# Expert rounds of 96 token places in place of 128, in a one-core decoder step on Trainium2

## The chip, the cores and the metric

The kernel runs on one core of one Trainium2 chip. The core has a matmul engine (TensorE, "PE" in the profile, its weight loads "PEld"), a vector engine (VectorE, "DVE"), a scalar engine (ScalarE, "ACT"), GpSimd ("POOL") and the engine that issues most of the transfers (SyncE, "SP"); 16 DMA engines move the data. The metric is the device time of one execution in microseconds, the median of three runs.

## What is computed

One inference step of a two-layer decoder, in float32, for 256 prompt tokens and 8 sample tokens (264 in all), model width 1024. Layer 0 is a gated DeltaNet mixer and a dense SwiGLU; layer 1 is a short gated convolution and a top-2-of-8 expert SwiGLU. The change is in the experts:

```python
def moe_swiglu(x, w_router, w_gu, w_down):
    logits = (x @ w_router).astype(jnp.float32)            # (tokens, 8)
    top_v, top_i = lax.top_k(logits, 2)
    gates = jax.nn.softmax(top_v, axis=-1)
    combine = jnp.einsum('...k,...ke->...e', gates, jax.nn.one_hot(top_i, 8, dtype=jnp.float32))
    y = jnp.zeros_like(x)
    for e in range(8):                                      # w_gu[e]: 1024 x 7168, w_down[e]: 3584 x 1024
        y = y + swiglu(x, w_gu[e], w_down[e]) * combine[..., e:e + 1].astype(x.dtype)
    return y
```

Each token goes to two experts, so an expert serves 66 tokens on average. The router of this reference, evaluated on its inputs, sends 68, 81, 87, 70, 66, 53, 45 and 58 tokens to the eight experts.

## The kernel before

Every weight matrix is streamed once, in slots of 128 x 2048 floats (1 MB). SP loads a slot into one of seven buffers (`raw`, line 360); ACT rounds it to the matmul format (`high`, line 367); DVE takes the remainder (`low`, line 372) over the raw data. A product is then three matmuls: high weights by high data, high by low, low by high. PE's `slot_used` semaphore gives the buffers back.

In layer 0 and in the convolution the weights are the stationary operand and all 264 tokens (266 columns) stream past. In the experts it is turned round: the tokens are the stationary operand (128 x CAP) and the weights stream past, 512 columns at a time.

The expert part works in *rounds*. A round gives each expert CAP places, CAP = 128; the number of rounds is read from the largest token count (`most`, lines 1632 to 1639: one, plus one if it is above CAP, plus one if above 2 CAP), and every round runs all eight experts. One expert in one round is a *job*: 42 slots, the same instruction stream on each engine, looped over with `Fori`, with the last job written out. The order inside a job is fixed by hand. A job has seven units of 512 hidden features (`UNITS`). For each unit PE does

- `gate_or_up` twice (lines 2279 to 2296): 48 matmuls, stationary `xgh` or `xgl` (128 x CAP), moving `high` or `low` (128 x 512), result in banks 0 to 3,
- `transpose_hidden` (line 2303): four transposes of `hx` (CAP x 128 each) into bank 6 or 7, the data as stationary operand and the identity as moving operand; they stand between the gate and the up half of the next unit,
- `down` (lines 2306 to 2327): 24 matmuls, stationary a CAP-column slice of `hth` or `htl`, moving `high` or `low`, accumulated in banks 4 and 5.

ACT applies silu (`sgx`, line 1061) and copies the transposed hidden tile (`hth`, line 1055); DVE multiplies (`hx`, line 1720) and takes the remainder (`htl`, line 1710). Near the end of a job `transpose_rows` (line 2260) transposes the next expert's tokens, eight transposes of `xrow`; DVE (`xf`, line 1644; `xgl`, line 1650) and ACT (`xgh`, line 1044) prepare them.

Tokens reach their places in two ways. For the first expert a one-hot matrix is built on DVE (line 1610) and 24 products with `xn` gather the columns (line 2268, each recorded as two matmuls). For the others POOL scatters rows into a DRAM table `tok` of 26 blocks of CAP rows (line 708), which SP reads back block by block (line 531). SP also stores each job's result `ysb` there (line 526). The 26 blocks are set to zero in layer 0 by transfers that POOL issues (line 610). After the last job POOL gathers each token's two results, except those of the last expert, which are taken from SBUF by a product with `final_ohT`.

## Time and profile before

| | us |
|---|---|
| median of three runs (1536.56 to 1539.73) | 1537.85 |
| span of the profiled execution | 1533.9 |
| PE busy in it | 1512.4 (99%) |
| PE weight loads busy | 1323.3 |
| DVE busy | 1274.1 (83%) |
| ACT busy | 1036.4 (68%) |
| POOL busy | 110.7 |
| mean granted clock of TensorE | 0.999 of full speed |

The span runs from the first to the last instruction of the profiled execution; the 3.95 us between it and the median lie around it. The experts run from about 561 us to about 1514 us of the span. In the timeline a line such as "x4" merges four neighbouring instructions: its start is that of the first and its length runs to the end of the last. The length of a single matmul includes the time until its result is out; neighbouring matmuls overlap. What one costs in a stream is the distance from its start to the start of the next.

### The profile page before, as it was taken

Reading aid. Unit: us, or ns where it says so; the run is one execution under the profiler, and the core shown is the slowest. Engines: PE = TensorE matmul, PEld = TensorE weight load, DVE = VectorE, ACT = ScalarE, POOL = GpSimd, SP = SyncE. Lnnn points to the kernel's source line nnn. Section 1 sums busy time; section 2 is a strip of 40 time slices with the busy share of each in tenths; the row PEclk is TensorE's granted clock in tenths of the full one; section 3 lists DMA queues with packets and bytes.
Section 4 is the critical chain, followed back from the end, with each engine's and each line's share of the span. In section 5 each row is a group of like instructions: output and inputs, shape, how many; then the busy total and the mean of one; then the engine's idle time right before and its main releaser. Section 6 shows DMA issues by size and latency. Waiting matters only on the chain.

```text
span 1533.9 us, 24252 instructions
## 1 busy us (share of the span) xinstructions
PE 1512.4 (99%) x9241; PEld 1323.3 (86%) x9241; DVE 1274.1 (83%) x1328; ACT 1036.4 (68%) x974; POOL 110.7 (7%) x171
## 2 busy tenths in 40 slices
PE   9999999999999999999999999999999999999997
PEld 8899999999999988888888888888888888888885
DVE  6986557796458779999899889889889889889896
ACT  6872546665344457777778778778778778777773
POOL 4313000120030120000000000000000000002100
PEclk9999999999999999999999999999999999999999
DMA  9968026896555559999999999999999999999991
GB/s 310 354 231 309 3 97 193 273 318 212 190 180 180 167 189 400 379 364 395 384 358 392 386 363 381 393 371 381 386 376 377 388 372 375 389 374 368 411 409 57
DMA packets 228140, 476.80 MB, mean 311 GB/s; under 512 B 10165, under 2 KB 69669, under 8 KB 227770
## 3 DMA queue, kind: packets, MB, share of 16 engines
q1 hardware_dynamic: 216216, 435.66, 77.9%
q0 software_dynamic: 11856, 40.19, 7.4%
q8 instruction: 48, 0.79, 0.2%
q14 instruction: 20, 0.16, 0.0%
HBM read 449.80 MB, written 26.24 MB: 310 GB/s over the span
## 4 chain that ended last, share of the span: by engine, by line
PE 90%; DVE 5%; ACT 3%; issue 2%; DVEq 0%; ACTq 0%
PE bank L2295 13%; PE bank L2291 12%; PE bank L2292 12%; PE bank L410 12%; PE bank L2320 11%; PE bank L416 6%; PE bank L2326 6%; PE bank L2156 3%; DVE low L372 2%; PE bank L2303 2%; PE bank L2161 1%; ACT high L367 1%; DVE xf L1644 1%; PE bank L423 1%; PE bank L432 1%
## 5 line engine op out<-in xcount | busy, mean ns | idle before, releaser
L372 DVE TENSOR_TENSOR low<-raw,high 128x2048 fp32r<-128x2048 f32 x404 | 919.9, 2292 | 142.4 <-ACT high L367 139.1
L367 ACT ACTIVATE high<-raw 128x2048 fp32r<-128x2048 f32 x404 | 773.6, 1918 | 284.3 <-PE bank L2295 89.0
L2291 PE MATMUL bank<-high,xgh 128*128 128x512 f32 x896 | 354.2, 395 | 0.4 <-DVE xgl L1650 0.4
L2292 PE MATMUL bank<-high,xgl 128*128 128x512 f32 x896 | 350.1, 391 | 0.0
L2295 PE MATMUL bank<-low,xgh 128*128 128x512 f32 x896 | 241.4, 392 | 1.4 <-DVE low L372 1.1
L2295 PEld LDWEIGHTS bank<-low,xgh 128*128 128x128 f32 x896 | 167.7, 188 | 40.3 <-DVE low L372 5.2
L2291 PEld LDWEIGHTS bank<-high,xgh 128*128 128x128 f32 x896 | 168.6, 188 | 34.2 <-issue 0.5
L2292 PEld LDWEIGHTS bank<-high,xgl 128*128 128x128 f32 x896 | 168.5, 188 | 33.8
L410 PE MATMUL bank<-xhb,high 128*128 128x266 f32 (+1 forms) x752 | 155.6, 288 | 2.0 <-DVE utail L1196 1.9
L410 PE MATMUL bank<-xlb,high 128*128 128x266 f32 (+1 forms) x752 | 153.9, 286 | 0.0
L2320 PE MATMUL bank<-high,hth 128*128 128x512 f32 x448 | 139.6, 393 | 0.0
L2320 PE MATMUL bank<-high,htl 128*128 128x512 f32 x448 | 138.2, 390 | 0.0
L410 PEld LDWEIGHTS bank<-xhb,high 128*128 128x128 f32 x752 | 117.3, 189 | 3.9 <-DVE utail L1196 2.1
L2326 PE MATMUL bank<-low,hth 128*128 128x512 f32 x448 | 120.0, 390 | 0.0
L410 PEld LDWEIGHTS bank<-xlb,high 128*128 128x128 f32 x752 | 117.6, 189 | 0.0
L416 PE MATMUL bank<-xhb,low 128*128 128x266 f32 (+1 forms) x752 | 101.7, 288 | 0.0
L2320 PEld LDWEIGHTS bank<-high,htl 128*128 128x128 f32 x448 | 84.2, 188 | 17.6
L2326 PEld LDWEIGHTS bank<-low,hth 128*128 128x128 f32 x448 | 84.1, 188 | 17.7 <-DVE low L372 0.2
L2320 PEld LDWEIGHTS bank<-high,hth 128*128 128x128 f32 x448 | 83.0, 188 | 16.3
L416 PEld LDWEIGHTS bank<-xhb,low 128*128 128x128 f32 x752 | 96.1, 190 | 1.1 <-issue 1.0
L722 POOL TENSOR_TENSOR flag<-flag 128x1 f32<-128x1 f32 x1 | 0.9, 873 | 840.7 <-DMA tok<-ysb 840.7
L1061 ACT ACTIVATE sgx<-bank 128x512 f32<-128x512 f32 x56 | 33.5, 598 | 38.4 <-PE bank L2295 38.2
(460 smaller groups left out, 1527.0 us busy)
## 6 DMA issues: line engine op xcount, KB each, us to landing
raw<-in_moe_w_gu_dram SPq DMA_DIRECT2D x224, 1024.0 KB, 5.6
raw<-in_moe_w_down_dram SPq DMA_DIRECT2D x112, 1024.0 KB, 6.0
raw<-in_ffn_w_gu_dram SPq DMA_DIRECT2D x22, 1024.0 KB, 5.6
raw<-in_gdn_w_in_dram SPq DMA_DIRECT2D x16, 1024.0 KB, 12.5
tok<-zeros POOLq DMA_DIRECT2D x26, 512.0 KB, 9.7
raw<-in_sc_w_in_dram SPq DMA_DIRECT2D x12, 1024.0 KB, 4.9
raw<-in_ffn_w_down_dram SPq DMA_DIRECT2D x11, 1024.0 KB, 5.5
s<-in_state_gdn_S_dram POOLq DMA_DIRECT2D x8, 512.0 KB, 8.0
```

Of the source, the lines that this page charges most:

```text
L367: eng.activation(high[:, n % SPLIT, :], raw[:, n % RAW, :], ACT.Copy).then_inc(high_ready, 1)
L372: eng.tensor_tensor(low[:, n % RAW, :], raw[:, n % RAW, :], high[:, n % SPLIT, :].bitcast(F32), ALU.subtract).then_inc(low_ready, 1)
L410: pe.matmul(out[t], wh[:, k, f[t]], act_[:, k, :], start=k == 0 and act_ is act_h, stop=False)
L416: last = pe.matmul(out[t], wl[:, k, f[t]], act_h[:, k, :], start=False, stop=k == KT - 1)
L1061: act.activation(sgx[:, u % 2, :], bank[2 * (u % 2)][:, :], ACT.Silu).then_inc(sgx_ready, 1)
L2156: pe.matmul(bank[d][:, 0:N], wh[:, k, 128 * d:128 * d + 128], act_[:, f + k, :], start=f + k == 0 and act_ is hh, stop=False)
L2291: pe.matmul(out, xgh[:, 4 * kh + k, :], wh[:, k, :], start=kh + k == 0, stop=False)
L2292: pe.matmul(out, xgl[:, 4 * kh + k, :], wh[:, k, :], start=False, stop=False)
L2295: last = pe.matmul(out, xgh[:, 4 * kh + k, :], wl[:, k, :], start=False, stop=kh == 1 and k == 3)
L2303: last = pe.transpose(bank[6 + u % 2][:, 128 * q:128 * q + 128], hx[:, u % 2, 128 * q:128 * q + 128], idn)
L2320: pe.matmul(bank[4 + g][:, :], src[:, u % 2, hs], wh[:, k, 512 * g:512 * g + 512], start=u + kh + k == 0 and src is hth, stop=False)
L2326: last = pe.matmul(bank[4 + g][:, :], hth[:, u % 2, hs], wl[:, k, 512 * g:512 * g + 512], start=False, stop=u == UNITS - 1 and kh + k == 2)
```

## The change

CAP goes from 128 to 96. Tiles that have a token on their partitions lose their last 32 partitions, tiles that have a token on their columns have 96 of them, and the transposes take a 96 x 96 identity. The number of rounds follows from the same comparison, now with 96 and 192. There are still at most three rounds, so 24 job blocks and two spare ones in `tok`.

```diff
-CAP = 128
+CAP = 96
 TILES = -(-N // CAP)
...
-        hx = place("hx", [128, 2, 512], at=region + 24 * D)
-        sgx = place("sgx", [128, 2, 512], at=region + 28 * D)
-        hth = place("hth", [128, 2, 512], F32R, at=region + 32 * D)
-        htl = place("htl", [128, 2, 512], F32R, at=region + 36 * D)
-        ysb = place("ysb", [128, D], at=region + 40 * D)
-        xrow = place("xrow", [128, D], at=region + 44 * D)
+        hx = place("hx", [CAP, 2, 512], at=region + 24 * D)
+        sgx = place("sgx", [CAP, 2, 512], at=region + 28 * D)
+        hth = place("hth", [128, 2, 4 * CAP], F32R, at=region + 32 * D)
+        htl = place("htl", [128, 2, 4 * CAP], F32R, at=region + 36 * D)
+        ysb = place("ysb", [CAP, D], at=region + 40 * D)
+        xrow = place("xrow", [CAP, D], at=region + 44 * D)
...
                     pool.dma_start(tok[j].rearrange("p (h f) -> p h f", h=4),
-                                   zeros[:, :].rearrange("p (o f) -> p o f", o=1).to_broadcast([128, 4, 256])).then_inc(zero_out, 16)
+                                   zeros[0:CAP, :].rearrange("p (o f) -> p o f", o=1).to_broadcast([CAP, 4, 256])).then_inc(zero_out, 16)
...
-                    act.activation(hth[:, u % 2, :], bank[6 + u % 2][:, :], ACT.Copy).then_inc(hth_ready, 1)
+                    act.activation(hth[:, u % 2, :], bank[6 + u % 2][:, 0:4 * CAP], ACT.Copy).then_inc(hth_ready, 1)
...
-                            act.activation(sgx[:, u % 2, :], bank[2 * (u % 2)][:, :], ACT.Silu).then_inc(sgx_ready, 1)
+                            act.activation(sgx[:, u % 2, :], bank[2 * (u % 2)][0:CAP, :], ACT.Silu).then_inc(sgx_ready, 1)
...
-                    ins = dve.tensor_scalar(xf[:, d, :], heads(2 + g)[:, d % 4, :], vecs[:, d, 2:3], vecs[:, d, 6:7],
+                    ins = dve.tensor_scalar(xf[:, d, :], heads(2 + g)[:, d % 4, 0:CAP], vecs[:, d, 2:3], vecs[:, d, 6:7],
                                             ALU.mult, ALU.add)
...
-                    dve.tensor_tensor(htl[:, u % 2, :], bank[6 + u % 2][:, :], hth[:, u % 2, :].bitcast(F32),
+                    dve.tensor_tensor(htl[:, u % 2, :], bank[6 + u % 2][:, 0:4 * CAP], hth[:, u % 2, :].bitcast(F32),
                                       ALU.subtract).then_inc(htl_ready, 1)
...
-                        last = pe.transpose(heads(2 + g)[:, d, :], xrow[:, ds], idn)
+                        last = pe.transpose(heads(2 + g)[:, d, 0:CAP], xrow[:, ds], ident[0:CAP, 0:CAP])
...
-                        last = pe.matmul(heads(2 + g)[:, d % 4, :], xn[:, tt, 128 * d:128 * d + 128], onehot[:, tt, :],
+                        last = pe.matmul(heads(2 + g)[:, d % 4, 0:CAP], xn[:, tt, 128 * d:128 * d + 128], onehot[:, tt, :],
                                          start=tt == 0, stop=tt == 2)
...
-                    out = bank[2 * (u % 2) + w][:, :]
+                    out = bank[2 * (u % 2) + w][0:CAP, :]
...
-                        last = pe.transpose(bank[6 + u % 2][:, 128 * q:128 * q + 128], hx[:, u % 2, 128 * q:128 * q + 128], idn)
+                        last = pe.transpose(bank[6 + u % 2][:, CAP * q:CAP * q + CAP], hx[:, u % 2, 128 * q:128 * q + 128],
+                                            ident[0:CAP, 0:CAP])
...
-                            hs = slice(256 * kh + 128 * k, 256 * kh + 128 * k + 128)
+                            hs = slice(CAP * (2 * kh + k), CAP * (2 * kh + k) + CAP)
                             for src in (hth, htl):
                                 for g in range(2):
-                                    pe.matmul(bank[4 + g][:, :], src[:, u % 2, hs], wh[:, k, 512 * g:512 * g + 512],
+                                    pe.matmul(bank[4 + g][0:CAP, :], src[:, u % 2, hs], wh[:, k, 512 * g:512 * g + 512],
                                               start=u + kh + k == 0 and src is hth, stop=False)
```

The tiles `onehot`, `xf`, `xgh`, `xgl`, `final_oh` and `seat` have CAP columns by their declarations, so they shrink with the constant.

## Rows read from the trace of the kernel before

**Rows 1.** The page, busy time by engine: us, share of the span, instructions.

```profile
PE 1512.4 (99%) x9241; PEld 1323.3 (86%) x9241; DVE 1274.1 (83%) x1328; ACT 1036.4 (68%) x974; POOL 110.7 (7%) x171
```

**Rows 2.** Windows in the experts: us, busy (instructions) by engine, granted clock, DMA share, GB/s.

```profile
1000.00:1100.00 100.00, 99.95 (x456) 82.53 (x455) 90.99 (x59) 77.28 (x53) 0.00 (x0) 1.00 1.02 381
```

**Rows 3.** Waits of PE, 560 to 1500 us: who waited for whom, us, times, longest.

```profile
PE bank L2295 <- DVE low L372: 1.1, 2, 0.6
PE bank L2291 <- DVE xgl L1650: 0.4, 1, 0.4
```

**Rows 4.** Waits of the load queue and of ACT, 600 to 1500 us.

```profile
SPq L360 <- PE bank L2295: 448.3, 210, 2.9
SPq L360 <- PE bank L2326: 232.8, 106, 3.0
...
ACT high L367 <- DMA raw<-in_moe_w_gu_dram: 5.2, 8, 0.7
```

**Rows 5.** Timeline of PE, a slot of gate_or_up: start us, length us, instruction, forms.

```profile
1014.10 0.39 PE L2291 MATMUL bank<-high,xgh 128*128 128x512 f32 x1
...
1015.91 1.07 PE L2295 MATMUL bank<-low,xgh 128*128 128x512 f32 x4
1016.82 0.39 PE L2291 MATMUL bank<-high,xgh 128*128 128x512 f32 x1
```

**Rows 6.** Groups by form, weight loads: rows*columns of the load, count, busy us, mean ns.

```profile
L2291 PEld LDWEIGHTS bank<-high,xgh 128*128 128x128 f32 x896 | 168.6, 188 | 34.2 <-issue 0.5
...
L1971 PEld LDWEIGHTS bank<-T,AT 64*64 64x64 f32 x320 | 9.9, 135 | 1.2 <-issue 1.0 <-ACT Kn L873 0.2
...
L1912 PEld LDWEIGHTS bank<-xhb,wabh 128*40 128x40 f32 x8 | 0.9, 114 | 0.1
```

**Rows 7.** Timeline of PE, 264 columns past a stationary operand 40 wide.

```profile
19.46 0.28 PE L1912 MATMUL bank<-xlb,wabh 128*40 128x264 f32 x1
...
22.12 0.29 PE L1912 MATMUL bank<-xhb,wabl 128*40 128x264 f32 x1
```

**Rows 8.** The same past a stationary operand 128 wide.

```profile
539.13 0.28 PE L423 MATMUL bank<-yh,high 128*128 128x264 f32 x1
...
540.73 0.28 PE L424 MATMUL bank<-yl,high 128*128 128x264 f32 x1
```

**Rows 9.** Timeline of PE around one transpose_hidden, and what follows it.

```profile
1018.64 1.07 PE L2295 MATMUL bank<-low,xgh 128*128 128x512 f32 x4
1019.55 0.60 PE L2303 MATMUL bank<-ident,hx 128*128 128x128 f32 x4
1019.90 0.48 PE L2291 MATMUL bank<-high,xgh 128*128 128x512 f32 x1
1020.22 0.40 PE L2292 MATMUL bank<-high,xgl 128*128 128x512 f32 x1
```

**Rows 10.** The chain of work, pieces of the two kinds of transposes: start us, us.

```profile
671.51 0.44 PE bank L2303 x4
...
674.72 0.87 PE bank L2260 x8
```

**Rows 11.** Transposes of 11 stationary columns by 128 moving ones: timeline, then its loads.

```profile
233.96 1.91 PE L2119 MATMUL bank<-ident,utail 128*11 128x128 f32 x16
...
L2119 PEld LDWEIGHTS bank<-ident,utail x24: 91/93/93, 233.7 to 358.1; 128*11 128x11 f32 x24
L2119 PE MATMUL bank<-ident,utail x24: 270/273/273, 234.0 to 358.2; 128*11 128x128 f32 x24
```

**Rows 12.** Transposes of 128 stationary columns by 28 moving ones: timeline, then one.

```profile
17.71 1.67 PE L1906 MATMUL bank<-ident,taps_nat 28*128 28x28 f32 x24
...
L1906 PE MATMUL bank<-ident,taps_nat x24: 217/218/240, 17.7 to 19.2; 28*128 28x28 f32 x24
```

**Rows 13.** One line's instructions: the token transposes of seven jobs, and the hidden ones.

```profile
L2260 PE MATMUL bank<-ident,xrow x56: 270/273/273, 674.6 to 1389.0; 128*128 128x128 f32 x56
...
L2303 PE MATMUL bank<-ident,hx x224: 269/272/277, 578.6 to 1505.2; 128*128 128x128 f32 x112
```

**Rows 14.** Timeline, start of the experts: the gather, and DVE, ACT and PE behind it.

```profile
555.31 5.62 PE L2268 MATMUL bank<-onehot,xn 128*128 128x128 f32 x48
...
559.70 0.63 ACT L1044 ACTIVATE xgh<-xf 128x512 fp32r<-128x512 f32 x1 [4.38 <-DVE xf L1644]
560.36 0.69 DVE L1650 TENSOR_TENSOR xgl<-xf,xgh 128x512 fp32r<-128x512 f32 x1 [0.70 <-ACT xgh L1044]
560.98 1.37 DVE L1644 TENSOR_SCALAR xf<-bank,vecs 128x128 f32<-128x128 f32 x4
...
561.29 0.49 PE L2291 MATMUL bank<-high,xgh 128*128 128x512 f32 x1 [0.36 <-DVE xgl L1650]
```

**Rows 15.** Timeline of PE: float32 matmuls with 8 moving columns, no transposes.

```profile
548.96 1.23 PE L2202 MATMUL bank<-gbw,xres 128*128 128x8 f32 x16
550.12 3.25 PE L2212 MATMUL bank<-high 128*128 128x512 f32 x13
```

**Rows 16.** Groups by form, DVE and ACT, of the hidden tile.

```profile
L1710 DVE TENSOR_TENSOR htl<-bank,hth 128x512 fp32r<-128x512 f32 x56 | 38.2, 682 | 0.0
...
L1055 ACT ACTIVATE hth<-bank 128x512 fp32r<-128x512 f32 x56 | 33.3, 595 | 9.9 <-PE bank L2303 9.9
```

More of the change, by code:

```diff
@@ L247, in hybrid_step @@
         final_oh = place("final_oh", [128, 3, CAP], at=region + 90 * D)
-        final_ohT = place("final_ohT", [128, N], at=tab_at + 4864)
+        final_ohT = place("final_ohT", [CAP, N], at=tab_at + 4864)
         quarters = place("quarters", [128, 3, 4, 6], at=region + 90 * D + 1600)
@@ L253, in hybrid_step @@
         SROWS = 4 * NS
-        seat_win = place("seat_win", [128, 40], at=mask_at)
+        seat_win = place("seat_win", [CAP, 40], at=mask_at)
         row_win = place("row_win", [128, 40], at=mask_at + 160)
@@ L1068, in expert @@
                         act.wait_ge(y_stored, job * 16 + 16)
-                        act.activation(ysb[:, 0:512], bank[4][:, :], ACT.Copy).then_inc(y_sb, 1)
+                        act.activation(ysb[:, 0:512], bank[4][0:CAP, :], ACT.Copy).then_inc(y_sb, 1)
                     if not last or i + SPLIT < EXPERT_SLOTS:
@@ L1719, in expert @@
                             dve.wait_ge(sgx_ready, units + (u + 1))
-                            dve.tensor_tensor(hx[:, u % 2, :], sgx[:, u % 2, :], bank[2 * (u % 2) + 1][:, :],
+                            dve.tensor_tensor(hx[:, u % 2, :], sgx[:, u % 2, :], bank[2 * (u % 2) + 1][0:CAP, :],
                                               ALU.mult).then_inc(hx_ready, 1)
@@ L1728, in expert @@
                             dve.wait_ge(ohT_psum, 1)
-                            step(dve.tensor_copy(final_ohT[:, :], bank[2][:, 0:N]))
+                            step(dve.tensor_copy(final_ohT[:, :], bank[2][0:CAP, 0:N]))
                             step(dve.tensor_copy(seat_win[:, 0:SROWS].rearrange("p (b d) -> p b d", d=4)[:, :, 3:4],
-                                                 bank[2][:, NP:N].rearrange("p (b o) -> p b o", o=1)))
+                                                 bank[2][0:CAP, NP:N].rearrange("p (b o) -> p b o", o=1)))
                             step.wait()
@@ L1736, in expert @@
                         dve.wait_ge(y_stored, job * 16 + 16)
-                        dve.tensor_copy(ysb[:, 512:1024], bank[5][:, :]).then_inc(y_sb, 1)
+                        dve.tensor_copy(ysb[:, 512:1024], bank[5][0:CAP, :]).then_inc(y_sb, 1)
                     if not last or i + SPLIT < EXPERT_SLOTS:
@@ L2323, in down @@
                         for k in range(2):
-                            hs = slice(256 * kh + 128 * k, 256 * kh + 128 * k + 128)
+                            hs = slice(CAP * (2 * kh + k), CAP * (2 * kh + k) + CAP)
                             for g in range(2):
-                                last = pe.matmul(bank[4 + g][:, :], hth[:, u % 2, hs], wl[:, k, 512 * g:512 * g + 512],
+                                last = pe.matmul(bank[4 + g][0:CAP, :], hth[:, u % 2, hs], wl[:, k, 512 * g:512 * g + 512],
                                                  start=False, stop=u == UNITS - 1 and kh + k == 2)
@@ L2345, in expert @@
                         n_tok = 128 if tt < 2 else NS
-                        last = pe.transpose(bank[2][:, 128 * tt:128 * tt + n_tok], final_oh[0:n_tok, tt, :], ident[0:n_tok, 0:n_tok])
+                        last = pe.transpose(bank[2][0:CAP, 128 * tt:128 * tt + n_tok], final_oh[0:n_tok, tt, :], ident[0:n_tok, 0:n_tok])
                     last.then_inc(ohT_psum, 1)
```

## The prediction

> **What bounds the kernel now.** I read the page first: PE is busy for 99% of the span, the next engine for 83% [rows 1]. A pipelined matmul counts as busy until its result is out, so that share doesn't say that PE is at its peak. The windows over the experts are alike from 600 to 1500 us: PE 99.95, DVE 91, ACT 77, granted clock 1.00, which is the 2.4 GHz level [rows 2]. The list of waits settles it: between 560 and 1500 us PE stood still for 1.5 us in all [rows 3]. The load queue, in contrast, waits for PE to give slots back for 681 us, and ACT waits only 5.2 us for the gate and up weights [rows 4]. So in the experts only the time that PE spends in its own instructions counts. A saving on DVE, ACT or in the transfers is worth nothing there by itself.
>
> What one instruction costs is the distance between starts. A gate slot has 12 matmuls of 512 columns and runs from 1014.10 to 1016.82, 2.72 us: 227 ns each [rows 5]. At 2.4 GHz 512 columns are 213 ns, so 14 ns are lost per matmul. A job has 42 such slots: 504 x 0.227 = 114.4 us. The job period is 118.9 us: from 674.6 to 1389.0 are seven groups of eight token transposes [rows 13], less the 0.76 us inside one group (seven distances of 0.109), over six periods. The rest, about 4.5 us, is 28 + 8 transposes and a little slack.
>
> **How many rounds.** The number of jobs comes first. The largest token count is 87, which is below 96, so there is one round of eight jobs as before. The 224 hidden transposes are 8 x 28 [rows 13]: one round today.
>
> **The large matmuls.** All 4032 (8 x 504) keep their 512 moving columns; only the stationary operand is narrower. Its load gets shorter: 188 ns at 128 columns, 135 at 64, 114 at 40 [rows 6], a line of 0.83 ns a column, so about 161 ns at 96. But the load runs beside the matmul ahead of it, and 188 is already less than 227. Does the lost 14 ns depend on the width? I compare 264 moving columns: past 40 stationary columns, 22 distances from 19.46 to 22.12, 121 ns [rows 7]; past 128, 13 distances from 539.13 to 540.73, 123 ns [rows 8]. Two ns for 88 columns is 0.7 ns for 32 columns, or 2.9 us over 4032 matmuls. I take 0 and keep 2.9 us as the bound on the gain side. On the loss side, the slices of stationary operand now begin every 384 bytes instead of 512. The 40-column slices begin every 160 bytes and cost nothing extra, so I take 0 there too, with 0.5 ns (2 us) as the bound.
>
> The Trainium skill, "TensorE: Matmul & The Clock Gate", section "LDWEIGHTS (loading the stationary operand)", says that a load takes P / 1.2 ns with P the columns; the slope of 0.83 in [rows 6] agrees. If the loads were exposed, that would be an estimated 27 ns on each of 4032 matmuls, over 100 us. They aren't, by the 227 ns of [rows 5].
>
> **The transposes.** Here the moving operand is the identity, so its width goes from 128 to 96. The stationary operand stays 128 columns wide (now 96 rows deep). Which of the two sets the time? First what one costs: one group of four starts at 1019.55, and the second matmul behind it at 1020.22; without the group that matmul would be 0.227 us behind, so four transposes cost 0.44 us [rows 9]. The chain of work gives the same 0.44, and 0.87 for eight [rows 10]: 109 ns each. With 11 stationary columns and 128 moving, 16 take 1.91 us; less the 0.273 us of the last one, that is 15 distances of 109 ns [rows 11]. So the narrow load changed nothing. With 128 stationary and 28 moving, 24 take 1.67 us; less 0.218, that is 23 distances of 63 ns [rows 12]. So the load (or another floor) stands at 63 ns, and above it the moving columns decide: 109 ns for 128 is 0.85 ns a column, near two cycles of 2.4 GHz (0.83). At 96 columns: 96 x 0.83 = 80 ns, and the remaining 2 ns, so 82 ns, above the floor of 63. The saving is 27 ns each. In the path stand 8 x 28 = 224 and 7 x 8 = 56 of them [rows 13]: 280 x 0.027 = 7.5 us. The bounds: a straight line between the two measured points (63 at 28, 109 at 128) has 94 ns at 96 columns, a saving of 15 ns or 4.1 us; if the load decided at full width the saving would be 0. I take 7.5, since the row with the 11 stationary columns has the same 109.
>
> The Trainium skill, same page, section "Back-to-back issue gap", gives N / 2.4 + 2.5 ns for a warm matmul, one cycle a column. By it a transpose would cost 56 ns now and 42 after, and 280 of them save an estimated 3.7 us. The 109 ns of [rows 10, 11] speak against it for float32 transposes.
>
> **The start of the experts.** The gather is 48 matmuls whose moving one-hot has 96 columns after the change. They cost (5.62 - 0.28) / 47 = 114 ns each [rows 14], where 0.28 is an estimate for the length of the last one, near the 0.27 of a transpose [rows 13]. Their stationary operand is float32 and 128 wide, and not a transpose. 16 matmuls of that kind, some with a narrower load, run from 548.96 to 550.12, 73 ns each, though only 8 columns stream past [rows 15]. So a full-width load sets at least 73 ns there, and may set all of the 114. The bounds for the 48 are 0 and 48 x 27 ns = 1.3 us; I take 0, because the loads stay at full width. Behind it PE waits 0.36 us for `xgl` [rows 14]. Four `xf` (1.37 us), `xgh` (0.63) and `xgl` (0.69) work on 96 of 128 columns each; a quarter of the streaming part, about 0.1 us of each, comes off, so that wait goes: 0.36 us. The 0.6 us wait for `low` a few slots later [rows 3] hangs on the same DVE queue, which is ahead by two such sets then, some 0.6 us; I take half, 0.3. Sum for the start: 0.7 us, bounds 0 and 2.3.
>
> **What costs nothing, and its cover.** `hth` on ACT (595 ns) and `htl` on DVE (682 ns) [rows 16] stream 384 in place of 512 columns and get shorter by a hundred ns or so, 56 times each; the matmuls between the transposes and `down` cover them entirely today (neither is among PE's waits [rows 3]), and they still do with a group of transposes that is 0.11 us shorter. `sgx`, `hx` and `ysb` have fewer partitions and the same columns, so the same time. The zeroing, the stores of `ysb` and the reads of `xrow` carry 384 KB in place of 512 KB; PE waits for none of them. No wait is added on any queue, and nothing is moved past anything else. Should the cover of the transfers fail, the wait of ACT for weights would grow from its 5.2 us [rows 4]; PE asks for each slot 0.8% sooner.
>
> **The sum.** 7.5 + 0.7 = 8.2 us off the span of 1533.9, hence 1525.7; the 3.95 us around it stay, and the median goes from 1537.85 to 1529.6, 0.5% less.
>
> **The rivals.**
>
> *A. The load holds the transposes.* At full width of both operands load and stream could be equally long, and only the load stay. For it: the load is still 128 columns. Against it: 63 ns with 128 stationary columns [rows 12]. Gain 0.7 us, time 1537.1. Chance 7%.
>
> *B. A transposed column costs less than I take.* Either a floor rises with the width (the straight line above, 4.1 us), or the 32 columns cost what a column of a large matmul does: 227 / 512 = 0.44 ns [rows 5], 14 ns for 32, 280 x 0.014 = 4.0 us. For it: no row has 96 moving columns. Against it: 0.85 ns a column at 128 [rows 11]. Gain 4.0 + 0.7, time 1533.1. Chance 8%.
>
> The back-to-back rule of the Trainium skill quoted above is this case.
>
> *C. Slower: the large matmuls pay for the odd slices.* Place: weight loads of `xgh`, `hth` and the like, at 384-byte steps, and results that fill 96 of 128 partitions. Each ns is 4.0 us, so 2 ns cancel the gain, and from 2.8 ns (11.3 us) it is slower by over 0.2%. At 4 ns: 16.1 - 8.2 = 7.9 us slower, time 1545.8. Against it: no penalty at 160-byte steps [rows 7]. Chance 4%.
>
> *D. A second round.* Price 8 x 118 = 944 us, time about 2470, decided by one expert above 96 tokens. With 87 it needs the kernel's routing to differ in ten places. Chance 1%.
>
> *E. The gain is absorbed.* DMA share is 1.02 at 381 GB/s [rows 2]; if that were the ceiling, PE would wait for weights as much as it saves. Against it: the queue's 681 us of waits [rows 4]. Time 1537.8. Chance 4%.
>
> *F. The large matmuls gain too*, up to 0.7 ns: gain up to 8.2 + 2.9, time 1526.7. Chance 8%.
>
> **How the numbers follow.** The forecast has 68%. Faster by over 0.2% (3.1 us, about what a measurement of this kernel can tell from no change): forecast, B and F, 84%, less 2% for runs that differ among themselves by 0.1% or so: 82%. Within 0.2%: A, E and these 2%, and 1% from a small C: 14%. Slower: 4%, C's larger part and D. The range reaches down to F, less 1 us: 1526. Upward it takes in B and the spread of the runs: 1534.5. A, C, D and E stay out, 16%.
>
> **What would show it.** Transposes on line 2303: four in the path cost 0.33 us in place of 0.44, and eight on line 2260 0.66 in place of 0.87. The job period goes from 118.9 to 118.0. A gate slot is still 2.72 us; loads on line 2291 have a mean near 161 ns. PE's wait for `xgl` is gone. The prediction is wrong if the group of four stays at 0.44 (A), if it comes to 0.38 (B), if a gate slot is off 2.72 by 0.03 or more (C, F), or if there are 16 jobs (D).

## The result, and the profile after

The changed kernel takes 1542.19 us (median of ten runs, 1540.66 to 1544.45) against 1537.35 of the kernel before (ten runs beside them, 1534.95 to 1539.77): ratio 1.0033, 95% interval 1.0024 to 1.0041. It is slower by some 5 us where 8 us less were forecast, and lies outside the stated range. Among the runs behind the numbers below, one of the six of the second experiment (1865.1 us) and one of the kernel before (1582.6 us) had a low granted clock, 0.751 and 0.90; the ratios leave them out, and without the first the median of the second experiment is 1526.99 us in place of 1527.32.

The page of the changed kernel; it answers to [rows 1]. It has the same number of instructions, so there is still one round of eight jobs.

```profile
span 1538.9 us, 24252 instructions
...
PE 1519.0 (99%) x9241; PEld 1211.1 (79%) x9241; DVE 1263.4 (82%) x1328; ACT 1028.2 (67%) x974; POOL 111.5 (7%) x171
```

DVE, ACT and the weight loads all have less to do, as the diff says, and PE is busy for longer. PE doesn't wait more than before; its waits between 560 and 1500 us have become shorter than [rows 3], and this is the only one left:

```profile
PE bank L2295 <- DVE low L372: 0.5, 1, 0.5
```

So the time went into PE's own instructions. The transposes did what was forecast. The chain of work of the changed kernel, the two kinds of transposes, beside [rows 10]:

```profile
663.87 0.33 PE bank L2303 x4
...
675.64 0.66 PE bank L2260 x8
```

0.33 in place of 0.44 and 0.66 in place of 0.87. The groups by form of the changed kernel show the weight loads with the forecast mean of 161 ns:

```profile
L2291 PEld LDWEIGHTS bank<-high,xgh 128*96 128x96 f32 x896 | 144.4, 161 | 60.7
```

Its token transposes, by line, run from 675.5 to 1393.9:

```profile
L2260 PE MATMUL bank<-ident,xrow x56: 243/246/247, 675.5 to 1393.9; 96*128 96x96 f32 x56
```

The job period is (1393.9 - 675.5 - 0.58) / 6 = 119.64 us against 118.94 before, by the same sum (a group of eight is 7 x 0.083 = 0.58 long now). It grew by 0.70 us where it should have shrunk by 0.97. The timeline shows where, in a gate slot as in [rows 5]:

```profile
1017.07 0.39 PE L2291 MATMUL bank<-high,xgh 128*96 128x512 f32 x1
...
1019.85 0.39 PE L2291 MATMUL bank<-high,xgh 128*96 128x512 f32 x1
```

The slot takes 2.78 us in place of 2.72: 231.7 ns for each of its 12 matmuls, with the same 512 moving columns, 5.0 ns more than the 226.7 of the slot before. The average over a job is less. Of the 3967 distances between neighbouring large matmuls in each trace, those up to 245 ns (all but 84 before and 67 after, which stand at transposes and waits) have a mean of 227.4 ns before and 231.4 after: 4.0 ns, or 16 us over 4032 matmuls. That is the size of rival C, which had 4%. What the narrow, shifted loads do to the stream is the subject of the experiments.

There is a second, smaller surprise, in the other direction. Before, the first slot of a job was late. The timeline of the kernel before, DVE and then PE at the change of jobs:

```profile
676.63 2.63 DVE L1644 TENSOR_SCALAR xf<-bank,vecs 128x128 f32<-128x128 f32 x8
679.18 1.47 DVE L1650 TENSOR_TENSOR xgl<-xf,xgh 128x512 fp32r<-128x512 f32 x2
680.57 4.48 DVE L372 TENSOR_TENSOR low<-raw,high 128x2048 fp32r<-128x2048 f32 x2
...
680.89 0.39 PE L2291 MATMUL bank<-high,xgh 128*128 128x512 f32 x1
...
682.48 0.39 PE L2292 MATMUL bank<-high,xgl 128*128 128x512 f32 x1
682.91 1.20 PE L2295 MATMUL bank<-low,xgh 128*128 128x512 f32 x4
683.94 0.39 PE L2291 MATMUL bank<-high,xgh 128*128 128x512 f32 x1
```

The slot takes 3.05 us, 0.33 more than its neighbours: between 682.48 and 682.91 PE waits for `low`, which DVE delivers late after eight `xf` and two `xgl`. The list of waits doesn't count this, since the long record of the matmul before covers the gap. The same place in the changed kernel:

```profile
677.44 2.37 DVE L1644 TENSOR_SCALAR xf<-bank,vecs 128x96 f32<-128x96 f32 x8
679.73 1.23 DVE L1650 TENSOR_TENSOR xgl<-xf,xgh 128x384 fp32r<-128x384 f32 x2
...
681.68 0.39 PE L2291 MATMUL bank<-high,xgh 128*96 128x512 f32 x1
...
684.46 0.39 PE L2291 MATMUL bank<-high,xgh 128*96 128x512 f32 x1
```

2.78 us, an ordinary slot of that kernel. DVE's work there is 0.5 us shorter and the stall of 0.3 us is gone.

The account of one job, in us: transposes -0.97, stall -0.3, and so the 504 large matmuls must bring +0.70 + 0.97 + 0.3 = +2.0, which is 3.9 ns each and agrees with the 4.0 of the distances. Eight jobs give 8 x 0.70 = 5.6 us; the spans differ by 5.0.

### The profile page after: what moved, and what is told of

Its sections match the earlier page's. It is cut to its first block, busy times and chain, and to the rows that moved or that the text cites. A ratio compares the mean times of both kernels' runs of the same rounds, so it can differ in the third digit from the quotient of the medians.

```text
span 1538.9 us, 24252 instructions
## 1 busy us (share of the span) xinstructions
PE 1519.0 (99%) x9241; PEld 1211.1 (79%) x9241; DVE 1263.4 (82%) x1328; ACT 1028.2 (67%) x974; POOL 111.5 (7%) x171
## 4 chain that ended last, share of the span: by engine, by line
PE 95%; DVE 2%; ACT 2%; issue 1%; DVEq 0%; ACTq 0%
PE bank L2321 13%; PE bank L2295 13%; PE bank L2291 13%; PE bank L2292 13%; PE bank L410 12%; PE bank L2327 7%; PE bank L416 6%; PE bank L2156 3%; PE bank L2161 1%; PE bank L2303 1%; PE bank L423 1%; PE bank L432 1%; PE bank L1971 1%; PE bank L424 1%; PE bank L2001 1%; ACT high L367 1%
## 5 line engine op out<-in xcount | busy, mean ns | idle before, releaser
L2291 PE MATMUL bank<-high,xgh 128*96 128x512 f32 x896 | 356.1, 397 | 0.0
L2292 PE MATMUL bank<-high,xgl 128*96 128x512 f32 x896 | 352.1, 393 | 0.0
L2295 PE MATMUL bank<-low,xgh 128*96 128x512 f32 x896 | 243.8, 394 | 0.5 <-DVE low L372 0.5
L2295 PEld LDWEIGHTS bank<-low,xgh 128*96 128x96 f32 x896 | 144.2, 161 | 62.1 <-DVE low L372 0.9
L2291 PEld LDWEIGHTS bank<-high,xgh 128*96 128x96 f32 x896 | 144.4, 161 | 60.7
L2292 PEld LDWEIGHTS bank<-high,xgl 128*96 128x96 f32 x896 | 144.8, 162 | 59.9
L2321 PE MATMUL bank<-high,hth 128*96 128x512 f32 x448 | 141.0, 396 | 0.0
L2321 PE MATMUL bank<-high,htl 128*96 128x512 f32 x448 | 139.7, 393 | 0.0
L2327 PE MATMUL bank<-low,hth 128*96 128x512 f32 x448 | 121.9, 394 | 0.0
L2327 PEld LDWEIGHTS bank<-low,hth 128*96 128x96 f32 x448 | 72.2, 161 | 31.7
```

The lines of the kernel that those rows point to most:

```text
L2291: pe.matmul(out, xgh[:, 4 * kh + k, :], wh[:, k, :], start=kh + k == 0, stop=False)
L2292: pe.matmul(out, xgl[:, 4 * kh + k, :], wh[:, k, :], start=False, stop=False)
L2295: last = pe.matmul(out, xgh[:, 4 * kh + k, :], wl[:, k, :], start=False, stop=kh == 1 and k == 3)
L2321: pe.matmul(bank[4 + g][0:CAP, :], src[:, u % 2, hs], wh[:, k, 512 * g:512 * g + 512], start=u + kh + k == 0 and src is hth, stop=False)
L2327: last = pe.matmul(bank[4 + g][0:CAP, :], hth[:, u % 2, hs], wl[:, k, 512 * g:512 * g + 512], start=False, stop=u == UNITS - 1 and kh + k ...
```

## The experiments

The theories. **W**: a load of fewer than 128 columns (or its result on fewer partitions) makes a matmul longer. **P**: the 384-byte step of the slices does. **T**: something else that became shorter or moved. The diffs show a few of the changed lines, with the run's constants for the step and the width of a load written out as numbers. The job periods below are all from the rows of the token transposes, by the sum above (with 0.76 for a group where the transposes have 128 columns).

**First: slices 512 bytes apart again, loads of 96 columns.**

```diff
-        hth = place("hth", [128, 2, 4 * CAP], F32R, at=region + 32 * D)
+        hth = place("hth", [128, 2, 512], F32R, at=region + 32 * D)
...
-        xgh = place("xgh", [128, KT, CAP], F32R, at=xs_at)
+        xgh = place("xgh", [128, KT, 128], F32R, at=xs_at)
...
-                            hs = slice(CAP * (2 * kh + k), CAP * (2 * kh + k) + CAP)
+                            hs = slice(128 * (2 * kh + k), 128 * (2 * kh + k) + 96)
```

> The changed kernel, but the slices of xgh, xgl, hth and htl begin every 512 bytes again (128 columns apart), while 96 columns of each are loaded. Three theories on the 3 ns or so that each large matmul of the experts costs more in the changed kernel (a gate slot of 12: 2.72 us before, 2.78 after). Theory W, the narrow load or the narrow result: nothing changes, a gate slot stays near 2.77 us, the time within 2 us of the changed kernel's 1542. Theory P, the 384-byte step of the slices: the slot goes back to 2.72 us and the time to 1542 - 13 = 1529. Theory T, something else that became shorter or moved (the work of DVE and ACT on 96 columns, the transposes): no change, 1542.

Measured: 1535.1 us (ten runs), ratio to the kernel before 0.9985 (0.9976 to 0.9994). The timeline has a gate slot of 2.76 us, 230.0 ns a matmul, and the job period is (1389.4 - 675.0 - 0.58) / 6 = 118.97.

```profile
1014.66 0.39 PE L2292 MATMUL bank<-high,xgh 128*96 128x512 f32 x1
...
1017.42 0.39 PE L2292 MATMUL bank<-high,xgh 128*96 128x512 f32 x1
```

Its token transposes, by line:

```profile
L2261 PE MATMUL bank<-ident,xrow x56: 243/246/246, 675.0 to 1389.4; 96*128 96x96 f32 x56
```

The result lies between the two theories (1542 by W, 1529 by P): the step costs 7 us of the time, and 3.3 ns a matmul remain in this slot with it gone.

**Second: the same, with loads of all 128 columns.** The last 32 are set to zero once, by POOL, and PE waits for that before the first job.

```diff
-                            pe.matmul(out, xgh[:, 4 * kh + k, :], wh[:, k, :], start=kh + k == 0, stop=False)
+                            pe.matmul(out, xgh[:, 4 * kh + k, 0:128], wh[:, k, :], start=kh + k == 0, stop=False)
```

> The changed kernel with slices 512 bytes apart and loads of the full 128 columns (the last 32 are set to zero once, and their results are never read); transposes, rounds and all work on DVE and ACT stay at 96. Theory W and theory P: the large matmuls are back at 227 ns, a gate slot at 2.72 us, and the transposes keep their saving of 7.5 us, so about 1530, faster than both kernels. Theory T: stays near 1542.

Measured: 1527.32 us (six runs), ratio 0.9933 (0.9920 to 0.9946): faster than both kernels. A gate slot is back at 2.72 us (1009.17 to 1011.89), 226.7 ns a matmul, with the short transposes kept:

```profile
1009.17 0.39 PE L2300 MATMUL bank<-high,xgh 128*128 128x512 f32 x1
...
1011.89 0.39 PE L2300 MATMUL bank<-high,xgh 128*128 128x512 f32 x1
```

Its token transposes, by line:

```profile
L2268 PE MATMUL bank<-ident,xrow x56: 244/246/248, 673.0 to 1380.2; 96*128 96x96 f32 x56
```

The job period is 117.77, that is 1.17 less than before: the 0.97 of the transposes and most of the stall. T is out: the work on DVE and ACT and the transposes are those of the changed kernel.

**Third: slices 384 bytes apart, loads of 128 columns** that run into the next slice.

```diff
-                            pe.matmul(out, xgh[:, 4 * kh + k, :], wh[:, k, :], start=kh + k == 0, stop=False)
+                            pe.matmul(out, xgh[:, 96 * (4 * kh + k):96 * (4 * kh + k) + 128], wh[:, k, :], start=kh + k == 0, stop=False)
```

> The changed kernel with slices 384 bytes apart as it has them, but loads of the full 128 columns (they run 32 columns into the next slice; those results are never read). PE waits for both halves of xgh and xgl before the first slot of a job, which costs up to 2.7 us at the start of the first job. Theory W: slot at 2.72 us, 1530 to 1533. Theory P: slot near 2.77 us, 1542 to 1545. Theory T: the same 1542 to 1545.

Measured: 1551.28 us (four runs), ratio 1.0092 (1.0076 to 1.0107). A gate slot is 2.80 us (1014.99 to 1017.79).

```profile
1014.99 0.40 PE L2298 MATMUL bank<-high,xgh 128*128 128x512 f32 x1
...
1017.79 0.63 PE L2328 MATMUL bank<-high,hth 128*128 128x512 f32 x2
```

This kernel was expected at 1530 to 1533 by W and at 1542 to 1545 by P, and is slower than either. So P holds also at full width, and costs more there than was expected: 0.08 us in this slot, 6.7 ns a matmul, and (1551.28 - 1527.32) / 4032 = 5.9 ns by the times, of which some 0.7 are the longer wait at the start (PE waits 2.66 us for `xgl` before the first job).

**Fourth: the kernel before with narrow loads and nothing else.**

```diff
-                    out = bank[2 * (u % 2) + w][:, :]
+                    out = bank[2 * (u % 2) + w][0:96, :]
...
-                            pe.matmul(out, xgh[:, 4 * kh + k, :], wh[:, k, :], start=kh + k == 0, stop=False)
+                            pe.matmul(out, xgh[:, 4 * kh + k, 0:96], wh[:, k, :], start=kh + k == 0, stop=False)
```

> The kernel before with one thing changed: the large matmuls of the experts load 96 of the 128 columns and write 96 partitions; all tiles, transposes, rounds and the work on DVE and ACT stay at 128. (Places 96 to 127 are empty in this data, so no token is left out.) Theory W: slot at 2.77 us or so, the time 1537.4 + 4032 x 0.0033 = 1550.7, slower than both kernels. Theories P and T: 1537.

Measured: 1544.8 us (four runs), ratio 1.0044 (1.0029 to 1.0059). Gate slot 2.76 us, job period (1399.0 - 677.6 - 0.76) / 6 = 120.11, which is 1.17 more than before, or 2.3 ns a matmul. W holds alone too. Eight periods make 9.4 us; the medians differ by 6.5, and the interval reaches to 9.1. That it is not the expected 13 has its reason in the averages: before, 13% of the distances up to 245 ns were above 228 already, with 128 columns, so their mean was 227.4 and not 226.7. It rose to 230.0, by 2.6 ns and not by 3.3.

**Fifth and sixth: the kernel before with loads of 112, and of 64 columns.** The edit is the fourth one with another number.

> The kernel before (all slices 512 bytes apart), with the large matmuls of the experts loading 112 of the 128 columns and writing 112 partitions (places 112 to 127 are empty in this data, no token is left out). With 96 of 128 the steady distance between matmuls was 230.0 ns, a slot 2.760 us, against 226.7 and 2.720 with 128. Theory step: any load below 128 columns costs the same 3.3 ns, so 230.0 ns and a job period of 120.1 us, about 1544. Theory slope: the cost grows with the columns left out, so 228.3 ns, 119.5 us, about 1541.

> As the run with 112 columns, with 64 of 128 loaded and written; the tokens in places 64 to 87 are left out of the gate, up and down products. Theory step: 230.0 ns, job period 120.1 us, about 1544. Theory slope: 3.3 ns for 32 columns, so 6.7 for 64: 233.3 ns, 121.8 us, about 1558.

Measured: 1548.8 and 1546.1 us (one run each beside 1535.2), job periods (1401.1 - 678.5 - 0.76) / 6 = 120.31 and (1398.9 - 677.6 - 0.76) / 6 = 120.09. The slope is out: in the job period, 16 columns fewer cost as much as 64 fewer. The times, of single runs, lie 2 to 5 us above the expected 1544. In one gate slot of the run with 112 columns the distance was 228.8 ns, near the 228.3 of the slope, but the mean over the run is 230.7: the steady distance alone doesn't give the time.

**Seventh and eighth: the kernel before, full loads, `xgh` and `xgl` begin 128, and 256, bytes later.**

```diff
-        xgh = place("xgh", [128, KT, CAP], F32R, at=xs_at)
-        xgl = place("xgl", [128, KT, CAP], F32R, at=xs_at + 4 * D)
+        xgh = place("xgh", [128, KT, CAP], F32R, at=xs_at + 128)
+        xgl = place("xgl", [128, KT, CAP], F32R, at=xs_at + 4 * D + 512 + 128)
```

> The kernel before with full loads of 128 columns; only xgh and xgl begin 128 bytes later, so that each of their slices of 512 bytes starts 128 bytes behind a 512-byte boundary and ends 128 behind the next. hth and htl stay where they are, so the down slots are a control in the same run: 2.720 us. Theory line: a load that starts off a 512-byte boundary costs more, about what the 384-byte step cost at full width (5 to 6 ns, gate slot 2.79), so 2688 x 0.006 = 16 us, about 1553. Theory step of 384: it is not the offset but the changing of it from slice to slice, and then a common offset costs nothing: 2.720 and 1537.

> As the run with 128 bytes, with 256 bytes. Theory line: as much as with 128 bytes, gate slot about 2.79 us, 1553. A variant of it: only offsets that are no multiple of 256 bytes cost, then 2.720 and 1537 here and the full price at 128. Theory step of 384: 2.720 us, 1537.

Measured: 1551.6 and 1539.6 us (one run each beside 1535.2). With 128 bytes, first a gate slot and then the second of two down slots in one timeline:

```profile
1014.65 0.40 PE L2291 MATMUL bank<-high,xgh 128*128 128x512 f32 x1
...
1017.45 0.63 PE L2320 MATMUL bank<-high,hth 128*128 128x512 f32 x2
...
1020.21 0.61 PE L2320 MATMUL bank<-high,hth 128*128 128x512 f32 x2
...
1022.93 0.40 PE L2291 MATMUL bank<-high,xgh 128*128 128x512 f32 x1
```

The gate slot takes 2.80 us, the down slot, whose tiles did not move, 2.72. The down slot before it takes 2.76 (1017.45 to 1020.21): the trouble runs on for some matmuls after its cause has ended. With 256 bytes the job period is (1392.3 - 677.8 - 0.76) / 6 = 118.96, that of the kernel before. So the variant of the line theory is right: slices that are off by 256 bytes are free, those off by 128 are not. Start and end of a load move together here; the ninth and the tenth experiment part them.

**Ninth: each price by itself.** Series of 24 matmuls on a weight slot, ahead of the experts, at a granted clock of 1.00. Between 556 and 640 us of this execution DVE and the transfers stand still and ACT is busy for 1 us. It is one execution, as are those of the second pair of series below.

```diff
             keep_dense(13, 3)
+            for i in range(24):
+                pe.matmul(bank[3][0:96, 0:512], block[:, 0:96], block[:, 1024:1536], start=True, stop=True)
...
+            for i in range(24):
+                pe.matmul(bank[3][0:96, 0:512], block[:, 32:128], block[:, 1024:1536], start=True, stop=True)
```

> The kernel before with 19 series of 24 matmuls each put in front of the experts, on a weight slot that is already there, into a bank whose contents nobody reads afterwards; it does more work than the kernel before (about 90 us), so only the distances inside a series count. They price one thing at a time: the load's columns (128, 112, 96, 64, 40), its start (0, 128 or 256 bytes behind a 512-byte boundary), the moving operand's columns (512, 384, 264) and its start (0 or 128 bytes). Theory by columns: with 512 moving columns 226.7 ns for 128, 230.0 for 96, 64 and 40, 232 to 233 for a start at 128 bytes, 226.7 for 256 bytes. With 264 moving columns, where the 40-column rows of the kernel before had 121 ns, the narrow load costs nothing (120 to 121 for 128, 96 and 40); that is why these rows did not show it. Rival: the cost is there at 264 columns too and the rows of before hid it in their scatter (then 118 for 128 and 121 for 96 and 40). Rival: the distances in this quiet stretch are all alike at 227, and the cost arises only beside the work of DVE, ACT and DMA in the experts.

The timeline of PE; a distance is the start of the next series less that of this one, over 24.

```profile
556.23 5.61 PE L2249 MATMUL bank<-high 128*128 128x512 f32 x24
561.68 5.69 PE L2251 MATMUL bank<-high 128*96 128x512 f32 x24
567.20 5.68 PE L2253 MATMUL bank<-high 128*64 128x512 f32 x24
...
594.83 5.60 PE L2263 MATMUL bank<-high 128*96 128x512 f32 x24
600.27 5.75 PE L2265 MATMUL bank<-high 128*128 128x512 f32 x24
605.86 3.05 PE L2267 MATMUL bank<-high 128*128 128x264 f32 x24
608.74 3.04 PE L2269 MATMUL bank<-high 128*96 128x264 f32 x24
611.62 3.06 PE L2271 MATMUL bank<-high 128*40 128x264 f32 x24
614.52 3.05 PE L2273 MATMUL bank<-high 128*128 128x264 f32 x24
...
631.34 5.76 PE L2281 MATMUL bank<-high 128*96 128x512 f32 x24
636.93 5.76 PE L2283 MATMUL bank<-high 128*128 128x512 f32 x24
```

128 columns cost 227 ns, 96 from byte 0 cost (567.20 - 561.68) / 24 = 230.0. The rival that the cost arises only beside the work of the other engines is out. With 264 moving columns all of them cost 120 to 121 ns, the 40-column load as well: the row that the prediction leaned on could not show the effect. And 96 columns from byte 128 (the series at 594.83) cost (600.27 - 594.83) / 24 = 226.7, nothing extra. So for 96 columns W is not about the width: the free load ends on a 512-byte boundary, the dear one at byte 384. A moving operand that starts at byte 128 costs too (the series at 600.27: 232.9). Loads of 40 columns missed their expectation: 233.3 in place of 230. And 128 columns from byte 256, which end at byte 768, cost (594.83 - 589.38) / 24 = 227.1, as expected, so 512 is not the only boundary. The series at 631.34 has the loads of the changed kernel, 96 columns each 384 bytes behind the last: (636.93 - 631.34) / 24 = 232.9, the dearest of the series with 96 columns, though it stands behind another dear one.

**Tenth: the changed kernel, 96 columns in the last three quarters of each 512-byte slice.** No padding, no full loads.

```diff
-                    act.activation(xgh[:, 4 * g:4 * g + 4, :], xf[:, 4 * g:4 * g + 4, :], ACT.Copy).then_inc(xgh_ready, 1)
+                    act.activation(xgh[:, 4 * g:4 * g + 4, 32:128], xf[:, 4 * g:4 * g + 4, :], ACT.Copy).then_inc(xgh_ready, 1)
...
-                            pe.matmul(out, xgh[:, 4 * kh + k, :], wh[:, k, :], start=kh + k == 0, stop=False)
+                            pe.matmul(out, xgh[:, 4 * kh + k, 32:128], wh[:, k, :], start=kh + k == 0, stop=False)
```

> The changed kernel with slices of xgh, xgl, hth and htl 512 bytes apart, and the 96 columns in the last three quarters of each (columns 32 to 127): each load still has 96 columns, but begins 128 bytes behind a 512-byte boundary and ends on one. Nothing is padded and no wait is added. The series priced this load at 226.7 ns, and the same 96 columns at the front of the slice at 230.0. Theory place (what counts is where the load lies against the 512-byte lines, not that it is narrow): gate slot back at 2.720 us, job period 117.8 us, about 1527, as fast as the version with full loads. Theory width (the series is not to be trusted beside the other engines' work, a narrow load costs 2 to 3 ns in the experts wherever it lies): slot 2.76 us, job period 119.0, 1535, as with the slices at the front.

Measured: 1528.21 us (six runs), ratio 0.9939 (0.9923 to 0.9954), job period (1383.0 - 675.9 - 0.58) / 6 = 117.75. Eight matmuls of a gate slot, and the token transposes:

```profile
1014.88 0.39 PE L2292 MATMUL bank<-high,xgh 128*96 128x512 f32 x1
...
1016.69 1.07 PE L2296 MATMUL bank<-low,xgh 128*96 128x512 f32 x4
...
L2261 PE MATMUL bank<-ident,xrow x56: 243/246/248, 675.9 to 1383.0; 96*128 96x96 f32 x56
```

(1016.69 - 1014.88) / 8 = 226 ns, and the mean of all distances up to 245 ns is 227.8, where the first experiment has 230.0. The same number of columns is loaded as in the first experiment, in 7 us less. The theory of the place is right, and W falls for loads of 96 columns: what it was credited with, 226.7 to 230.0, belongs to where the load ends.

**Eleventh and twelfth: where a load may begin and end.** Two more sets of series, the second with six free matmuls ahead of each series.

> The kernel before with 18 series of 24 matmuls of 512 columns in front of the experts (about 100 us more), each with another load: columns and start in bytes. Theory end: a load costs nothing extra (226.7 ns) when its last column ends on a 512-byte boundary, or on one of 256 bytes, wherever it begins: 96 from 128 and from 640, 64 from 256 and from 768, 112 from 64, 40 from 352, 32 from 384, 120 from 32, and 128 from 0 and 512; extra for 96 from 256, 64 from 128, 64 from 384, 127 from 0, 32 from 0, 128 from 384. 96 from 384 (ends on 256 behind a boundary) tells 512 from 256. Rival, length: only loads of a multiple of 128 bytes that end so are free, or only those of 384 and 512 bytes, and shorter ones cost even when they end on a boundary. Rival, start: the load from 128 bytes was free for its start, and then 64 and 32 columns from there are free too.

> As the series before, with six matmuls of the free kind (128 columns from byte 0) ahead of each of 15 series, so that each starts from the same state. In the last series 96 columns from byte 640 cost 231.6 ns although they end on a 512-byte boundary, but they came behind a series with the same pattern of distances, and the version with all its slices so placed runs at 227 to 228 ns. Theory state: the stream keeps the pattern it is in, and from the free state the 96 columns from 128, from 640 and from 384 (they end on 512, 1024 and 768) all stay at 226.7, while 96 from 0 goes to 230.0. Theory address: 96 from 640 and from 384 are at 231.6 again, whatever ran ahead. For narrow loads that end on a boundary (64 from 256, 32 from 384, 80 from 192, 100 from 112) the theory of the end says 226.7, the theory of the length 230.

The second set's timeline; the columns are in the form, the first byte is named below.

```profile
565.74 5.60 PE L2255 MATMUL bank<-high 128*96 128x512 f32 x24
571.18 1.52 PE L2257 MATMUL bank<-high 128*128 128x512 f32 x6
572.54 5.60 PE L2259 MATMUL bank<-high 128*96 128x512 f32 x24
577.98 1.52 PE L2261 MATMUL bank<-high 128*128 128x512 f32 x6
...
586.14 5.69 PE L2267 MATMUL bank<-high 128*96 128x512 f32 x24
591.67 1.53 PE L2269 MATMUL bank<-high 128*128 128x512 f32 x6
593.04 5.68 PE L2271 MATMUL bank<-high 128*64 128x512 f32 x24
598.56 1.52 PE L2273 MATMUL bank<-high 128*128 128x512 f32 x6
```

From byte 640 (it ends at 1024) and from 384 (768) 96 columns cost 5.44 / 24 = 226.7 ns; from byte 0 (384) 5.53 / 24 = 230.4; 64 columns from 256 (512) 5.52 / 24 = 230.0. All the free ones of the set: 96 from 128, 384, 640 and 896, 100 from 112, 112 from 64, 120 from 32, 80 from 192; each ends on a multiple of 256. Dear: 96 and 112 from 0, 128 from 128, which end elsewhere, and 64 and 32 that end on one. 127 from 0 (ends at 508) is free, though it was expected to cost. So neither the theory of the end nor that of the length holds whole: for loads of 80 columns and more the end decides, with 127 from byte 0 as an exception, and loads of 64 and 32 columns cost extra even where they end on a boundary. In the first set, 96 from 640 stood behind a dear series:

```profile
597.92 5.72 PE L2265 MATMUL bank<-high 128*96 128x512 f32 x24
603.48 5.68 PE L2267 MATMUL bank<-high 128*64 128x512 f32 x24
```

It cost (603.48 - 597.92) / 24 = 231.7: theory state is right, and 24 such loads did not bring the stream back to the pattern that they keep when they start in it. The six loads of 128 columns from byte 0 ahead of each series of the second set did, after at most four dear distances. This fits the changed kernel, in which only every second slice ends off a 256-byte boundary: 82% of its distances up to 245 ns are above 228 ns, and in the kernel before 13% were. But that the state carries the cost from slice to slice there is an inference. By the ends alone the changed kernel should pay less than the first experiment, where every slice ends off a boundary, and it pays more (means of 231.4 and 230.0 ns). Why the 384-byte step is dearer stays open.

## Why the prediction was wrong

*What bounds the kernel.* Right: PE's own instructions set the time, and all that moved it lies there. Too strict was "a saving on DVE is worth nothing there by itself": a stall of 0.3 us a job stood in the kernel before, and the shorter `xf` and `xgl` removed it. The list of waits had 1.5 us for PE and not these 2 us; a look at every distance above 227 ns would have shown it. The stall was part of the "little slack": 36 transposes of 0.109 us are 3.9 of the 4.5 us that the prediction had left over in a job.

*The count of rounds.* Right, one of eight jobs; rival D is out. So is E: PE waits less than before.

*The large matmuls.* This is the step that failed. "The 40-column slices begin every 160 bytes and cost nothing extra, so I take 0" carried a reading at 264 moving columns over to 512. The series show that at 264 every load is free (120 to 121 ns) and at 512 it is not. The term was 0 with bounds from -2.9 to +2 us; it measured about +16 us (8 x 504 x 3.9 ns). The gain side (rival F) rested on scatter: the 2 ns between [rows 7] and [rows 8] aren't there when 128, 96 and 40 columns are loaded side by side. Two parts are seen in the job periods: (118.97 - 117.75) / 504 = 2.4 ns for loads that end at byte 384 of a slice of 512 (first and tenth experiment), and (119.64 - 118.97) / 504 = 1.3 ns for the step of 384 bytes on top (changed kernel and first experiment), which the place of the ends alone doesn't explain. Rival C had the right place and the right sum ("each ns is 4.0 us"), and 3.9 ns lie next to its example of 4, which no row had given: that is luck. Its chance of 4% rested on the same row of 264 columns, and "odd slices" pointed at the 384-byte step, where for 96 columns the end of the load decides.

*The transposes.* Right to 0.01 us: 0.33 and 0.66 in place of 0.44 and 0.87, 7.6 us in all. The inference from the two rows with unlike operands [rows 11, 12] held: two cycles a column above a floor. Rivals A and B are out. The Trainium skill's formula of one cycle a column ("TensorE: Matmul & The Clock Gate", section "Back-to-back issue gap", for the isolated gap of a warm matmul: N / 2.4 + 2.5 ns) gives an estimated 42 ns at 96 columns. It does not hold for these float32 transposes: the trace has 83 ns between them.

*The start.* The gather cost what it did (48 matmuls in 5.6 us), as forecast, and the wait for `xgl` is gone. The first large matmul starts at 561.22 in place of 561.29, but the gather had begun 0.33 us later in this execution (555.64 and 555.31), so from there on the gain is 0.4 us, the forecast 0.36. The second wait is 0.5 us where it was 0.6, a gain of 0.1 where 0.3 were taken.

*The sum.* -7.6 for the transposes, -2 for the stall (seven changes of jobs), -0.5 for a wait for `low` in the last job, which the kernel before has between 1388 and 1514 us and the changed kernel hasn't, and +16 for the matmuls make +5.9. Measured are +5.0 between the spans, nearly all of it between the first and the last large matmul (952.6 us before, 957.6 after); the remaining 0.9 us is not assigned. The statement that 3.95 us lie around the span was wrong as well: the profiled executions of the later runs lie 1.7 to 2.0 us above their spans, so the profiled execution of the kernel before was one of the faster.

*The forecast gain exists*: with the loads placed well, the kernel is at 1527.3 or 1528.2, 10 us below before (the prediction: 1529.6). That the time is so near the forecast is in part luck: about 2 of the 10 us are the stall, which the forecast did not have.

## What to carry to other kernels

A narrower tile isn't only less work: it moves the addresses of everything behind it. Before the pitch of a stationary operand is changed, look where its loads end, keep slices 512 bytes apart, and put a narrow slice at their end. This is shown for 96 columns in the whole kernel and for 80 to 120 in the series. When a row is taken as evidence for a cost that a matmul has in a stream, it must have the same moving width; 4000 instructions turn 4 ns into more than the whole forecast gain. And look for the stall in the distances between starts, since the list of waits hides what a long matmul record covers.

## What the runs showed of the hardware

In a stream of matmuls of 512 columns whose loads run beside them (float32 in the matmul format, granted clock 1.00, the 2.4 GHz level), the distance is 226.7 ns if the load has 80 or more columns and ends on a multiple of 256 bytes, and 228.9 (112 columns from byte 0), 230.0 (96) or 232 to 233 (128 from byte 128) if it doesn't. These are some twenty places, each in a series of 24 matmuls in one execution, and one is an exception: 127 columns from byte 0, which end at byte 508, cost 226.7. Loads of 64, 40 and 32 columns cost 229 to 233 wherever they were put. With 384 moving columns 96 from byte 0 cost 175.0 against 173.3, with 264 nothing. A moving operand that starts at byte 128 costs 233. After a dear load the stream stays slow for a while: up to four matmuls when loads of 128 columns from byte 0 follow, and all 24 of a series when 96 columns do that end on a boundary (from byte 640, 231.7). Why this is so no run shows; it stays open, as does whether the narrow result or the narrow load makes the 64-column case dear.

In the best version PE waits for DVE in places. In the last job of the version with full loads, after DVE has added a row tile to `acc`, PE waits for `low`; the timeline has the distance from 1465.27 to 1466.12, 0.85 us in place of 0.23, twice in that job (the kernel before has one such wait in its last job):

```profile
1462.01 1.26 DVE L1712 SCALAR_TENSOR_TENSOR acc<-rows_a,gate_ab,acc 128x1024 f32<-128x1024 f32 x1
...
1465.27 0.39 PE L2301 MATMUL bank<-high,xgl 128*128 128x512 f32 x1
1466.12 1.20 PE L2304 MATMUL bank<-low,xgh 128*128 128x512 f32 x4 [0.46 <-DVE low L373]
```
